# Chunked recurrence: products in twos on diagonal and crossed 64x64 tiles, keys masked by GpSimd, own part of the mix on ScalarE

## The reference

```python
def _wkv7_scan(r, w, k, v, kk, a):
    # S_t = S_{t-1} diag(w_t) + (S_{t-1} (-kk_t)) (kk_t * a_t)^T + v_t k_t^T ;  o_t = S_t r_t
    ...
    def frame_step(S, inp):
        r_t, w_t, k_t, v_t, kk_t, a_t = inp
        sa = jnp.einsum('bhvk,bhk->bhv', S, -kk_t)
        S = (S * w_t[:, :, None, :]
             + sa[..., None] * (kk_t * a_t)[:, :, None, :]
             + v_t[..., None] * k_t[:, :, None, :])
        o_t = jnp.einsum('bhvk,bhk->bhv', S, r_t)
        return S, o_t
```

## Time and profile before

| | |
|---|---|
| median of 3 runs | 2493.17 us (2492.76 to 2497.76) |
| span of the profiled execution, first to last instruction | 2489.5 us |
| the profiled execution's own time | not on the page; it is told by its span |
| busy PE / DVE / ACT / POOL | 2433.6 / 1283.3 / 946.2 / 1118.5 us |
| share of PE in the chain that ended last | 90% |
| PE clock granted | 9 in tenths in each of 40 slices (9 is 90% or more) |
| DMA | 207.21 MB, mean 83 GB/s |

### The profile page before, as it was taken

How to read it: one execution, slowest core, us unless ns; L and a number is a source line. 1 busy time by engine, 2 the same in 40 slices (tenths; PEclk the granted TensorE clock), 3 DMA queues, 4 the chain that set the end, 5 groups by cost and what they waited for, 6 DMA issues and landing times.

```text
span 2489.5 us, 43675 instructions
## 1 busy us (share of the span) xinstructions
PE 2433.6 (98%) x16740; PEld 2004.7 (81%) x16740; DVE 1283.3 (52%) x2051; ACT 946.2 (38%) x1541; POOL 1118.5 (45%) x623
## 2 busy tenths in 40 slices
...
DMA packets 57997, 207.21 MB, mean 83 GB/s; under 512 B 6464, under 2 KB 9192, under 8 KB 57592
## 3 DMA queue, kind: packets, MB, share of 16 engines
...
q0 software_dynamic: 320, 1.05, 0.1%
...
HBM read 201.36 MB, written 3.70 MB: 82 GB/s over the span
## 4 chain that ended last, share of the span: by engine, by line
PE 90%; DVE 5%; ACT 2%; issue 1%; DMA 0%; POOL 0%; SPq 0%; DVEq 0%; ACTq 0%; POOLq 0%
PE banks L2022 25%; PE banks L2024 25%; PE banks L2023 24%; PE banks L2511 7%; PE banks L2266 1%; PE banks L2283 1%; PE banks L2574 1%; PE banks L2247 1%; PE banks L2242 1%; PE banks L2188 1%; PE banks L2418 1%; PE banks L2556 1%; PE banks L2251 1%; ACT sb_wh L485 0%; DMA sb_x<-xT 0%
## 5 line engine op out<-in xcount | busy, mean ns | idle before, releaser
L1878 POOL TENSOR_TENSOR sb_wl<-sb_raw,sb_wh 128x1024 fp32r<-128x1024 f32 (+1 forms) x366 | 888.1, 2429 | 999.3 <-ACT sb_wh L485 998.8
L2022 PE MATMUL banks<-sb_bh,sb_wh 128*128 128x512 f32 x2656 | 1049.4, 395 | 23.0 <-DVE sb_bl L1449 9.9
L2024 PE MATMUL banks<-sb_bh,sb_wl 128*128 128x512 f32 x2656 | 1038.2, 391 | 0.0
L2023 PE MATMUL banks<-sb_bl,sb_wh 128*128 128x512 f32 x2656 | 1036.8, 390 | 0.0
L2022 PEld LDWEIGHTS banks<-sb_bh,sb_wh 128*128 128x128 f32 x2656 | 500.5, 188 | 142.4 <-issue 28.6
L2024 PEld LDWEIGHTS banks<-sb_bh,sb_wl 128*128 128x128 f32 x2656 | 500.4, 188 | 107.3
L2023 PEld LDWEIGHTS banks<-sb_bl,sb_wh 128*128 128x128 f32 x2656 | 500.7, 189 | 104.6 <-issue 2.2
L485 ACT CAST sb_wh<-sb_raw 128x1024 fp32r<-128x1024 f32 (+1 forms) x366 | 376.7, 1032 | 492.0 <-PE banks L2024 486.6
L1112 DVE SCALAR_TENSOR_TENSOR sb_x<-sb_x,banks 128x512 f32 x72 | 49.6, 688 | 312.4 <-PE banks L2024 312.4
L1173 DVE TENSOR_TENSOR sb_bl<-sb_t,sb_bh 128x512 f32 x64 | 163.3, 2551 | 7.9
L2511 PE MATMUL banks<-sb_m 64*64 64x64 f32 (+1 forms) x3840 | 154.7, 234 | 1.4 <-DVE sb_m L1689 0.9
...
## 6 DMA issues: line engine op xcount, KB each, us to landing
...
```

The source lines that it names most:

```text
L1878: nc.gpsimd.tensor_tensor(wl[:, s, 0:cols], raw[:, s, 0:cols], wh[:, s, 0:cols].bitcast(F32), ALU.subtract).then_inc(lo_ready, 1)
L2022: nc.tensor.matmul(out, hi_a, hi_b, start=first, stop=False)
L2023: nc.tensor.matmul(out, hi_a, lo_b, start=False, stop=False)
L2024: return nc.tensor.matmul(out, lo_a, hi_b, start=False, stop=last)
```

## The change

Products that ACT moves are done by a new `crosswise`: two of them (or two groups of one) are interleaved, the first on the diagonal tiles, the second with each head's output on the other head's 64 partitions (the crossed tiles). ACT copies a crossed bank in two halves of 64 partitions, back to the right ones. So done are `lr.g` with `kr.g`, and `kt`, `at`, `vt`, `bt`, `w`, `tt` with group 0 diagonal and group 1 crossed; `z`, `t`, `x32` and `mp` stay with `product`. `kr` is now moved unmasked by ACT (four copies) and masked in place by POOL (`mk.0`, `mk.1`). ACT does the own part of the mix (`own_part`), DVE its third operation. On DVE `lr.0` and its first X come ahead of `lr.1`; V's mix and the bonus follow the transpose. The orders of PE, DVE, ACT and POOL inside `half` change; decay and rate run interleaved on the two halves of the rows; K's dense product is cut in 7 and 1 of 8.

```diff
+    def own_part(c, i, tile, done, own, dst):
+        b = tile_bank(c, tile)
+        act.wait_ge(panel_done, p0 + 4 * c + done)
+        mu = mu_own[:, NC * i + c:NC * i + c + 1]
+        nc.scalar.activation(dst[:, 0:1], psum[:, b, 0:1], ACT.Copy, scale=mu)
+        nc.scalar.activation(own, psum[:, b, :], ACT.Copy, scale=mu).then_inc(own_ready, 1)
+    def own_keys(c):
+        own_part(c, 1, 2, 1 if c else 2, kkn, zk)
...
         split(Idx(0, p0 + 4 * c + 5), 2 * P if c < NC - 1 else D)
+        own_part(c, 0, 3, 3, sq[:, 0, :], zr)
         if c:
             high(c - 1)
+        if c < NC - 1:
+            nc.scalar.activation(r8[:, 4, 0:1], eps[:, 0:1], ACT.Tanh)
         half(c)
...
+        def move(product, dst, crossed=(1,)):
+            for g in range(2):
                 st.wait(half_pe, n, f"{product}.{g}")
                 b_ = bank(f"{product}.{g}")
-                if isinstance(dst, tuple):
-                    ins = nc.scalar.copy(quad(g, *dst), b_.rearrange("p c (s n) -> p c s n", s=2))
-                else:
-                    ins = nc.scalar.copy(one(g, dst), b_)
+                for to, of in halves(g in crossed):
+                    if isinstance(dst, tuple):
+                        ins = nc.scalar.copy(quad(g, *dst)[to], b_[of].rearrange("p c (s n) -> p c s n", s=2))
+                    else:
+                        ins = nc.scalar.copy(one(g, dst)[to], b_[of])
                 st.did(half_act, f"{product}.{g}", ins)
         last = n == NC - 1
+        tile_moved(n, 3)
+        own_part(n, 2, 4, 4, sq[:, 0, :], zv)
+        move("kr", (M_AK, M_RK), (0, 1))
+        move("kt", M_KT)
+        move("at", M_AT)
+        move("z2", M_Z, ())
+        move("vt", M_VT)
+        move("z4", M_Z, ())
         if not last:
             decay_tanh(n + 1)
-        move("vt", M_VT)
-        move("z2", M_Z)
-        move("kt", M_KT, [0])
+        move("z8", M_Z, ())
         if not last:
             rate_tanh(n + 1)
-        move("kt", M_KT, [1])
-        move("z4", M_Z)
-        move("at", M_AT)
-        move("z8", M_Z)
         move("bt", M_BT)
-        move("z16", M_Z)
+        move("z16", M_Z, ())
         move("w", M_W)
-        move("z32", M_Z)
+        move("z32", M_Z, ())
         split(Idx(0, p0 + 4 * n + 6))
         move("tt", (M_TA, M_TW))
         if not last:
+            own_keys(n + 1)
             st.wait(half_pool, n, "dg")
             decays(n + 1)
-        if not last:
             key_square(n + 1)
             nc.scalar.activation(r8[:, 5, 0:1], eps[:, 0:1], ACT.Sqrt)
...
+    def mix(c, i, nth, tile, own, dst):
         b = (g0 + tile) % 2
-        dve.wait_ge(panel_done, p0 + 4 * c + done)
+        dve.wait_ge(own_ready, 3 * c + nth)
         k = NC * i + c
-        V.tensor_scalar(dst[:, 0:1], psum[:, b, 0:1], mu_own[:, k:k + 1], None, ALU.mult)
-        link(V.tensor_scalar(own, psum[:, b, :], mu_own[:, k:k + 1], None, ALU.mult))
         V.scalar_tensor_tensor(dst[:, 1:T], psum[:, b, 0:T - 1], pcol("mu_rkv", k), own[:, 1:T], ALU.mult,
                                ALU.add).then_inc(bank_free[b], 1)
         tile_moved(c, tile)
...
+        def masked_left(g):
             masks = wm[:, 0:2, :].unsqueeze(1).broadcast_to([P, 4, 2, 64])
-            grouped(name, lambda g: did(f"{name}.{g}", V.tensor_tensor(
-                quad(g, first, second), pair_of(bank(f"{name}.{g}")), masks, ALU.mult)))
+            st.wait(half_pe, n, f"lr.{g}")
+            did(f"lr.{g}", V.tensor_tensor(quad(g, M_LT, M_RB), pair_of(bank(f"lr.{g}")), masks, ALU.mult))
...
         def first_x(g):
             link(V.tensor_tensor(one(g, M_X), one(g, M_LT), each(wm[:, 3, :]), ALU.mult))
             did(f"x1.{g}", V.tensor_tensor(one(g, M_X), one(g, M_X), each(eye[:, :]), ALU.add))
-        masked("lr", M_LT, M_RB)
         st.wait(half_pool, n, "bd")
-        st.wait(half_dve, n, "lr.1")
-        first_x(0)
+        for g in range(2):
+            masked_left(g)
+            first_x(g)
+        turned(1)
+        mix(n, 2, 3, 4, sq[:, 0, :], zv)
         st.wait(pair_pe, n, "bonus")
         b = (g0 + 5) % 2
         V.scalar_tensor_tensor(sq[:, 1, :], psum[:, b, :], 64.0, zv, ALU.mult, ALU.mult).then_inc(bank_free[b], 1)
-        first_x(1)
-        turned(1)
-        masked("kr", M_AK, M_RK)
+        beside = {16: decay_exponent} if n < NC - 1 else {}
         if n:
-            output_low(n - 1)
-        beside = {8: decay_exponent, 16: decay_sums, 32: rates} if n < NC - 1 else {}
+            beside[4] = lambda _: output_low(n - 1)
         for b in LEVELS:
             if b != LEVELS[-1]:
...
+            decay_sums(n + 1)
+            rates(n + 1)
             mix_keys(n + 1)
...
+        def masked_right(g):
+            masks = wm[:, 0:2, :].unsqueeze(1).broadcast_to([P, 4, 2, 64])
+            st.wait(half_act, n, f"kr.{g}")
+            st.did(half_pool, f"mk.{g}", nc.gpsimd.tensor_tensor(
+                quad(g, M_AK, M_RK), quad(g, M_AK, M_RK), masks, ALU.mult))
+        off(0, 0)
         st.did(half_pool, "dg", nc.gpsimd.tensor_tensor(
             m_all[:, M_DG, :, :], eye[:, :].unsqueeze(1).broadcast_to([P, 8, 64]), last_decay, ALU.mult))
-        for i, b in enumerate(LEVELS):
-            for g in range(2):
-                if i == 0:
-                    st.wait(half_dve, n, f"lr.{g}")
-                else:
-                    st.wait(half_pe, n, f"z{LEVELS[i - 1]}.{g}")
-                st.did(half_pool, f"off{b}.{g}", nc.gpsimd.tensor_tensor(
-                    one(g, M_OFF), one(g, M_LT), each(wm[:, 4 + i, :]), ALU.mult))
+        off(0, 1)
+        masked_right(0)
+        off(1, 0)
+        off(1, 1)
+        masked_right(1)
+        for i in range(2, len(LEVELS)):
+            off(i, 0)
...
+        s = p % SLOTS
+        for i, (w_, h_) in enumerate(((wh, lh[0]), (wh, ll[0]), (wl, lh[0]))):
+            for e in range(2):
+                r = slice(64 * e, 64 * e + 64)
+                last = nc.tensor.matmul(psum[:, banks[e], :], w_[r, s, 0:P], h_[r, :], start=(i == 0), stop=(i == 2))
+                if i == 2:
+                    last.then_inc(panel_done if e and c == 0 else mid_done, 1)
...
+        def crosswise(first, second, needs=()):
+            for s, (name, a, b, ch0) in enumerate((first, second)):
+                i = PRODUCTS.index(name)
+                if i == 0:
+                    started(pe, n, half_act)
+                waits(list(needs) + ([MOVED[PRODUCTS[i - 6]]] if i >= 6 else []))
+            for j in range(4):
+                for e in range(2):
+                    r = slice(64 * e, 64 * e + 64)
+                    for s, (name, a, b, ch0) in enumerate((first, second)):
+                        ch, to = ch0 + j, (1 - e if s else e)
+                        out = bank(name)[64 * to:64 * to + 64, j, :]
+                        lhs = v_chunks[r, ch, :] if a is None else m_all[r, a, ch, :]
+                        if isinstance(b, tuple):
+                            rhs, out = m_all[r, both(*b), ch, :], out.rearrange("p (s n) -> p s n", s=2)
+                        elif b is None:
+                            rhs = centre[r, :] if a is None else eye[r, :]
+                        else:
+                            rhs = m_all[r, b, ch, :]
+                        last = nc.tensor.matmul(out, lhs, rhs, start=True, stop=True, skip_group_check=True)
+                        if j == 3 and e == 1:
+                            st.did(half_pe, name, last)
+        def all_chunks(name, a, b, needs=()):
+            crosswise((f"{name}.0", a, b, 0), (f"{name}.1", a, b, 4), needs)
...
             st.wait(post_dve, n - 1, "oinverse")
-        product("lr", [(M_B, (M_A, M_R))], needs=[by_dve("r")])
-        product("kr", [(M_K, (M_A, M_R))], needs=[by_dve("k")])
+        for g in range(2):
+            crosswise((f"lr.{g}", M_B, (M_A, M_R), 4 * g), (f"kr.{g}", M_K, (M_A, M_R), 4 * g), [by_dve("k")])
+        if n:
+            st.wait(post_dve, n - 1, "out")
+        all_chunks("kt", M_KD, None, [by_pool("kd")])
         bonus(n)
+        all_chunks("at", M_A, None)
+        def level(b):
+            product(f"z{b}", [(M_OFF, M_T)], needs=[by_pool(f"off{b}"), by_dve(f"t{b // 2}")])
+            product(f"t{b}", [(M_X, M_Z)], needs=[by_act(f"z{b}"), by_dve(f"x{b // 2}")])
+        level(2)
+        pe.wait_ge(bank_free[v_bank], n * 3 + (g0 + 4) // 2 + 1)
+        all_chunks("vt", None, None)
+        level(4)
         if n < NC - 1:
             decay_and_rate(n + 1)
-        if n:
-            st.wait(post_dve, n - 1, "out")
-        pe.wait_ge(bank_free[v_bank], n * 3 + (g0 + 4) // 2 + 1)
-        product("vt", [(None, None)])
-        def level(b, beside):
-            product(f"z{b}", [(M_OFF, M_T)], needs=[by_pool(f"off{b}"), by_dve(f"t{b // 2}")])
-            beside(0)
-            product(f"t{b}", [(M_X, M_Z)], needs=[by_act(f"z{b}"), by_dve(f"x{b // 2}")])
-            beside(1)
```

(30 more changed lines are left out.)

34 lines of the change are left out of this document (22 added, 12 removed).

## The result

The changed kernel takes 2496.57 us (median of 18 runs, 2494.26 to 2500.78) against 2491.97 of the kernel before in the same series: ratio 1.0018, interval 1.0012 to 1.0025. It is 4.6 us slower where 10 us less were forecast.

What follows compares the result with a forecast made beforehand. PE, with 90% of the chain in a 2489.5 us span, was taken as the bound. Legs summed to -1.10 a pair, seven pairs -7.7, pair 0 -2.2, together -9.9: time 2483, range 2473 to 2505.

Steps and rivals of the forecast that it cites:

- Four tiles for the time of two: PE's crossed products: crossed tiles run beside diagonal ones, four in the time of two, half of the old price.
- the walk: Step-by-step timing of the legs, with lr.1 and kr.1 done at 1.74 and z2 at 5.70; chance 0.45, 2477 to 2489.
- Rival B: Crossed tiles do not run beside diagonal ones: up to +1.95 a pair, pair 0 +0.85, time 2508; chance 0.13.
- Rival C: Only 128-wide products gain; 64-wide vt, bt, w keep their time: +1.40 a pair, time 2494; chance 0.08.
- Leg 1: From lr to z2: 5.70 us instead of 7.42, with DVE and GpSimd holding each other up.
- Rival A: GpSimd gets ahead of DVE's first X after lr.0's mask: leg 1 is 7.46, time 2497; chance 0.22.
- Leg 2: From z2 to the dense product of the next pair's keys: 13.87 us instead of 13.58, including 2.1 of stalls.
- Leg 3: From that dense product to the first carried state: 10.65 us instead of 10.32; bounds -0.2 and +1.7.
- Pair 0: First pair: 1.5 more to win at its late masks, less about 0.35 as lr waits for k; -2.2.
- Masking kr by GpSimd: kr's masks on GpSimd, 1.05 each, wanted only by w some 10 us later.

Runs made afterwards that it cites:

- run 3: Changed kernel, but GpSimd's off2 waits for the first X instead of the lr mask, and dg comes behind kr's masks: 2490.71 us, ratio 0.9995 to the kernel before.
- Run 1: Changed kernel, but ScalarE copies z4 ahead of vt, z16 ahead of bt, z32 ahead of w: 2484.69 us, ratio 0.9973 to the kernel before.
- Run 4: Changed kernel, but DVE does the own part of the keys' mix again, r and v staying with ScalarE: 2489.23 us, ratio 0.9989 to the kernel before.
- run 9: Changed kernel with z copied first, off2 and dg later, keys' own part on DVE, but no product crossed: 2495.32 us, ratio 1.0017 to the kernel before.

## Why the prediction was wrong

- **Four tiles for the time of two: right** (1.80 for lr and kr; half of 3.64 is 1.82, and not the 1.74 of the walk). Rival B falls. Rival C falls too: kt, 32 records of 64 columns, has the next start 0.57 after its own, where vt had 0.98. The rule of the Trainium skill (page "TensorE: Matmul & The Clock Gate", Part 3, what overlaps and what doesn't), that a weight load overlaps matmuls in flight only in another row group, is not what this trace shows: diagonal and crossed tiles share their rows, and 64 records go in 1.80. The loads of the earlier trace rows had shown only that loads overlap one another.
- **Leg 1, -1.72: right** (-1.70), collisions included; run 3 shows by itself what they cost, 0.93. Rival A gave 2497, near the measured time, for the wrong reason: DVE won the call. It started 0.04 ahead of GpSimd, not 0.02 behind. The Trainium skill (page "SBUF — State Buffer", section "Who interferes with whom") lets the first to issue go first, and this call agrees with it; the lead given to GpSimd was wrong.
- **Leg 2, +0.29: the step that failed** (+1.59). The mechanism was in the prediction, and its size was wrong: the term is the stall of "0.56" where "the three copies of a crossed product are still ahead", worked out from 0.27 more for a copy. Measured is 0.89 each (1.82 less the 0.93 of two groups). The copies of a crossed product start together, when both groups are done, and where the partitions change they are some 0.39 apart, not 0.27: of the 1.81 for five copies, 0.37 is the last one and 0.27 the step between z4's two, which leaves 1.17 for three steps. Three stalls of 0.33 more are 1.0 of the missing 1.3. The other 0.3 lies in the changes from one kind of product to the next, for which the prediction had 0.1 in all; from x32 to K's dense product, for one, it is 1.08 (1489.44 to 1490.52), not 0.93. Run 1 takes 1.38 back by the order of the copies alone. The prediction priced the wait and did not ask whether ScalarE's order had to be so.
- **Leg 3, +0.33: too small** (+0.87). tt's three copies are 0.60 apart, not 0.48, and the own part, with its column 0 ahead of it, takes 0.84 (1498.50 to 1499.34), not 0.6; so it ends 3.8 after tt, not 3.3. Run 4 shows what this one pass costs: 0.90.
- **Pair 0, -2.2:** it came to -0.8. Its legs fell by 2.16 (2.6 were forecast), and lr starts 1.38 later and not 0.35, a term that the prediction gives without its working. Of the 1.03 that are missing, the two stretched DVE passes are 0.77 (0.99 and 1.23 less 0.77 and 0.68); the prediction did not look for a collision with GpSimd there. That it is the wait for k, run 9 shows: its lr needs r alone and starts 0.32 after the start of the last record ahead of it, where the changed kernel's starts 1.8 after.
- For pair 1 this makes -1.70 + 1.59 + 0.87 = +0.76; against most later pairs it is about +0.9, since their leg 2 was 13.38 before and not 13.58. Pairs 1 to 6 lose 5.3 us together, where seven pairs were to win 7.7.
- The range held the measured time, and that was luck: the way that it moved was not the one forecast.
- Masking kr by GpSimd was costed at nothing. No wait on it shows in pair 1 (its second mask ends at 1478.77, w starts at 1487.04), but no run takes it away alone, so that stays argued.
